# Two changes in the attention stage of a fused two-block kernel: sums of squares placed later in the order, and an output projection summed in four parts

## What is computed

```python
proj = h @ w_in                                   # od_w_in: 2048 x 4608
q, k, v, gate = split(proj)                       # 32 query heads, 4 key heads of 64
q = rope(rms_norm_2(q, q_norm_w), pos)            # needs a sum of squares per token and head
k = rope(rms_norm_2(k, k_norm_w), pos)
o = swa_sinks(q, k, v, sinks)                     # attention over a window of 128, with sinks
return (o * silu(gate)) @ w_out                   # od_w_out: 2048 x 2048, added to x
```

## Time and profile before

| | before |
|---|---|
| median of three runs | 1874.39 us |
| the profiled execution | 1875.87 us |
| its span, first to last instruction | 1874.0 us |
| TensorE busy | 1862.7 us, 99% of the span |
| VectorE busy | 1246.1 us, 66% |
| ScalarE busy | 1002.7 us, 54% |
| mean granted TensorE clock | 0.998 |

### The profile page before, as it was taken

The page is one execution under the profiler, slowest core; times in us unless marked ns, Lnnn a source line. Parts: engine busy times, 40 slices in busy tenths (PEclk is TensorE's granted clock), DMA queues, the critical chain, the costliest instruction groups (busy, mean ns, idle before and its releaser), DMA issues.

```text
span 1874.0 us, 22288 instructions
## 1 busy us (share of the span) xinstructions
PE 1862.7 (99%) x8403; PEld 1534.2 (82%) x8403; DVE 1246.1 (66%) x1833; ACT 1002.7 (54%) x1422; POOL 35.8 (2%) x90
## 2 busy tenths in 40 slices
PE   9999999999999999999999999999999999999999
PEld 7888888888888888888888888888888888877777
DVE  6676566776666556665466776765676666776786
ACT  6677554554444344443444455564565545476763
POOL 0001000000000000000000000000000001001100
PEclk9999999999999999999999999999999999999999
DMA  9667764786666666666666686666666678677985
GB/s 324 202 194 179 207 183 151 215 257 192 195 193 193 193 191 191 193 197 196 189 198 194 201 281 203 192 191 190 185 203 198 193 238 241 202 234 216 268 255 174
DMA packets 223628, 388.36 MB, mean 207 GB/s; under 512 B 15696, under 2 KB 45184, under 8 KB 223520
## 3 DMA queue, kind: packets, MB, share of 16 engines
q1 hardware_dynamic: 222272, 384.17, 68.3%
q0 software_dynamic: 816, 2.11, 0.8%
q10 hardware_dynamic: 432, 0.66, 0.1%
HBM read 367.83 MB, written 19.05 MB: 206 GB/s over the span
## 4 chain that ended last, share of the span: by engine, by line
PE 95%; DMA 2%; DVE 1%; ACT 1%; SPq 0%; issue 0%; DVEq 0%; ACTq 0%
PE g L1341 31%; PE g L1342 30%; PE g L1343 30%; DMA PTB<-probs 1%; DMA queries<-TWQ 1%; DVE wl L1797 1%; PE ob L1404 1%; ACT wh L1513 0%; DMA queries<-TE 0%; DMA probs<-A 0%; PE m L1391 0%; PE m L1483 0%; DMA A<-queries 0%; PE m L1283 0%; DVE TWQ L1797 0%
## 5 line engine op out<-in xcount | busy, mean ns | idle before, releaser
L1797 DVE TENSOR_TENSOR wl<-raw,wh 128x1024 fp32r<-128x1024 f32 (+1 forms) x660 | 802.0, 1216 | 554.1 <-ACT wh L1513 551.0
L1513 ACT ACTIVATE wh<-raw 128x1024 fp32r<-128x1024 f32 (+1 forms) x661 | 695.2, 1053 | 750.2 <-PE g L1343 739.5
L1341 PE MATMUL g<-wh,xh 128*128 128x512 f32 x1886 | 740.7, 393 | 0.0
L1343 PE MATMUL g<-wh,xl 128*128 128x512 f32 x1886 | 735.6, 390 | 0.0
L1342 PE MATMUL g<-wl,xh 128*128 128x512 f32 x1886 | 735.6, 390 | 0.0
L1341 PEld LDWEIGHTS g<-wh,xh 128*128 128x128 f32 x1886 | 354.5, 188 | 78.4 <-issue 3.8
L1343 PEld LDWEIGHTS g<-wh,xl 128*128 128x128 f32 x1886 | 354.5, 188 | 74.1
L1342 PEld LDWEIGHTS g<-wl,xh 128*128 128x128 f32 x1886 | 354.6, 188 | 72.2
L1341 PE MATMUL g<-wh,mh 128*128 128x512 f32 x732 | 287.6, 393 | 0.4 <-issue 0.4
L1343 PE MATMUL g<-wh,ml 128*128 128x512 f32 x732 | 285.4, 390 | 0.0
L1342 PE MATMUL g<-wl,mh 128*128 128x512 f32 x732 | 285.3, 390 | 0.0
(11 more groups left out here) (175 smaller groups left out, 716.3 us busy)
## 6 DMA issues: line engine op xcount, KB each, us to landing
raw<-in_ev_w_in SPq DMA_DIRECT2D x128, 512.0 KB, 3.8
raw<-in_w_in SPq DMA_DIRECT2D x92, 512.0 KB, 4.4
raw<-in_w_gate SPq DMA_DIRECT2D x88, 512.0 KB, 4.4
raw<-in_w_up SPq DMA_DIRECT2D x88, 512.0 KB, 4.4
raw<-in_w_down SPq DMA_DIRECT2D x88, 512.0 KB, 4.8
raw<-in_od_w_in SPq DMA_DIRECT2D x72, 512.0 KB, 4.5
raw<-in_w_out SPq DMA_DIRECT2D x32, 512.0 KB, 4.2
raw<-in_ev_w_out SPq DMA_DIRECT2D x32, 512.0 KB, 4.8
```

The source lines that it names most:

```text
L1341: e.matmul(o, hi[:, kt, c], h, start=first, stop=False)
L1343: last = e.matmul(o, lo[:, kt, c], h, start=False, stop=end)
L1513: return e.activation(o, i, AF.Copy, scale=scale)
L1797: return e.tensor_tensor(o, a, b, op)
```

## The change

Sums of squares of quarter j: `on_sum` is put into the order only when the planned end of the earlier quarter's send is 1.5 us past. The output projection's first part, rows 0 to 7, becomes two parts, rows 0 to 3 and rows 4 to 7; the moving of units ahead, which the first part had, falls away. The same weights are loaded and the same products made; there are 16 blocks of two units in place of four of four and eight of two, and so 16 `add` steps in place of 12.

```diff
-    for kts in (every[:8], every[8:12], every[12:]):
+    for kts in (every[:4], every[4:8], every[8:12], every[12:]):
         for j in range(4):
             block("od_w_out", 0, 512 * j, 512, kts, "M5", "add", j, kts[-1] == KT - 1, 4)
...
-    for acts, n in (("X1", 12), ("M3", 8), ("X2", 12), ("X3", 12), ("M5", 4)):
+    for acts, n in (("X1", 12), ("M3", 8), ("X2", 12), ("X3", 12)):
...
                     for i in range(2):
+                        while a[0] and self.end[("qsend", a[0] - 1, i)] + 1.5 > self.now:
+                            yield 1
                         say("on_sum", a[0], i)
```

## The result

The changed kernel takes 1877.54 us as a median of 12 runs, the kernel before 1874.66 in the 12 runs beside it: ratio 1.0015, 95% interval 1.0008 to 1.0022, some 2.9 us slower. The forecast was 1873.5, and its range ended at 1876.8. The prediction called less than 0.2% no change; the interval shows a loss all the same, where a small gain was forecast.

A forecast was written before the change was run, and what follows sets the result against it. TensorE, 99% busy, was taken as the bound, with idle and half clock around `oapv` 1. 1875.87 - 6.9 + 2.8 + 2.95 + 0.3 = 1875.0, less 1.48 for the median: 1873.5 us; own range 1871.5 to 1876, wider 1867.4 to 1876.8.

The forecast's parts named there:

- What bounds the kernel: TensorE, 99% busy; idle time and half clock around `oapv` of group 1 worth 0.69 + 3.25 + 2.95 = 6.9 us.
- Part one: Moving `on_sum` of quarter 2 later lets group 1's send and fetch leave earlier, removing the `oapv` 1 stretch: 6.9 us gained.
- with what drains earlier and the load that now comes behind, I take 1699.5: Landing of group 1's fetch, taken down from 1701.2; no wait left at `oapv` 1, bounds 0 and 2.0 us.
- the ring order: Earlier issue gains only the DMA engines' idle time: group 1's fetch lands at 1702.1, wait 1.7 us, sum 1.7 higher.
- The line set as refutation: A wait at `oapv` 1 above 2 us would refute part one.
- Part two: Four output-projection parts: counted adds push `oapv` 7 directly ahead of unit 653; 2.8 us more wait, 2.95 clock, 0.3 `pfetch` 5.
- The second turn's six looks for room: Group 6's second probability turn fails six planner checks for VectorE backlog (at most 3 us), placed six units later, delaying `oapv` 7.
- The clock: Half clock behind the late wait at unit 653 costs 2.95 us, bounds 0 and 2.95.
- clock holds: Rival: the wait at unit 653 ends before the clock falls; 1870.6 us, chance 0.17.
- The 0.3 us for `pfetch` 5: Allowance because group 5's fetch now goes out behind an add: 0.3 us, bounds 0 to 1.3.
- The third rival: Transfers queue behind others, `pfetch` of group 1 lands after 1702.8, clock falls again at `oapv` 1; 1879.8 us, chance 0.10.
- The upper end of 1876.8: Top of the wider range, 1867.4 to 1876.8 us, reaching to the bounds of the unknown costs.

The follow-up runs named there:

- e8: The changed kernel again, unaltered, run and profiled a second time: 1876.03 us, ratio 1.0020 to the kernel before.
- e1: The kernel before with part one alone (the wait ahead of `on_sum`), output projection still in three parts: 1872.65 us, ratio 0.9987.
- e7: Part one alone, with the two weight loads ahead of group 1's fetch (units 610 and 611) halved to 256 KB: 1870.88 us, one run.
- e4: Part one alone, with send and fetch of group 1's probabilities earlier in SyncE's order: 1870.01 us, ratio 0.9973 to the kernel before.
- e12: Part one alone, with only the fetch of group 1 moved ahead of the loads of units 610 and 611: 1870.05 us, ratio 0.9979.
- e11: The kernel before again, unaltered, profiled a second time: 1873.06 us, one run.
- e3: The changed kernel, both parts, with the output projection's adds made but left out of the planner's VectorE clock: 1871.41 us, ratio 0.9985.
- e10: The changed kernel without one look for room on VectorE, that of the second turn of group 6: 1880.51 us, one run.
- e2: The kernel before with part two alone (four parts of the output projection), `on_sum` in its old place: 1879.57 us, ratio 1.0022.
- e6: The changed kernel with adds not counted by the planner, and sends and fetches of groups 1 and 3 earlier: 1869.81 us, ratio 0.9980.
- e13: The kernel before, neither part, with only the fetch of group 1 moved ahead of the two loads: 1871.91 us, ratio 0.9987.
- e9: The changed kernel with adds not counted by the planner, and sends and fetches of groups 1, 3 and 5 earlier: 1870.74 us, ratio 0.9979.

## Why the prediction was wrong

**What bounds the kernel: right in kind, too large in size.** The stretch around `oapv` 1 was the place. Its worth of 6.9 us came from one execution; the second profile gives 4.9. The same kernel's send of the queries took 6.55 us in the one and 5.24 in the other, and the half clock cost 2.95 and 1.71 us.

**Part one: the step that failed is "with what drains earlier and the load that now comes behind, I take 1699.5".** The ends before it held: the send at 1684.75 for 1685.1, the fetch at 1691.52 for 1692.2. The landing came at 1701.35 in the first profile of the changed kernel, 1701.32 in the second (e8) and 1701.33 in e1; the 1701.2 that the prediction had before that last deduction was within 0.2 us of it. No load comes behind: the loads of units 610 and 611 stand ahead of the fetch in SyncE's queue before and after, as the earlier trace rows shows (0.96, x2). The 9.0 us from issue to landing already held their bytes, and there was nothing to take off; it measured 9.83. e7, e4 and e12 put these loads at 2.2 to 3.0 us each.

What an earlier issue gained was at most about the time in which the DMA engines had stood idle. Windows of the kernel before in its first profile, then in its second, e11 (columns as in the earlier trace rows):

```profile
1684.00:1688.00 4.00, 3.29 (x20) 2.16 (x20) 1.29 (x2) 1.62 (x3) 0.00 (x0) 1.00 0.72 275
1688.00:1692.00 4.00, 4.00 (x20) 3.30 (x19) 3.49 (x4) 3.12 (x6) 0.00 (x0) 1.00 0.57 129
```

```profile
1684.00:1688.00 4.00, 4.00 (x24) 2.93 (x19) 3.38 (x4) 1.82 (x5) 0.00 (x0) 1.00 0.67 204
1688.00:1692.00 4.00, 4.00 (x20) 3.30 (x19) 1.40 (x2) 3.97 (x5) 0.00 (x0) 1.00 0.87 307
```

The shares leave 2.8 us idle in the first and 1.8 in the second, an estimate from 0.72 and 0.57, 0.67 and 0.87; in the changed kernel the same eight microseconds are full (1.04 and 1.09). The landing gained 2.9 us against the first (1704.27) and 0.7 against the second (1702.02). Both agree with what I had drawn from the ring order in the Trainium skill ("DMA: Bandwidth & Descriptors", section "Queues, rings and completion order"): by it, with 2.2 us of idle time, the landing was 1702.1 and the wait 1.7; measured were 1701.35 and 2.18. I had weighed this case and set it aside for a value that no row gave. The line set as refutation, a wait above 2 us at `oapv` 1, was passed. Part one was worth 2.4 us (0.7 to 4.1), not 6.9.

TensorE came at 1699.2, not 1700.4: of that, 1.1 us are the head start at `oapv` 0, which the change did not make. It lengthened the wait, but cost no time, as the landing sets when `oapv` 1 begins.

**Part two: right in mechanism, and in the size of the late wait.** The planner's count of the adds was the cause (e3), `oapv` 7 fell directly ahead of unit 653, and the wait was 3.17 us in three profiles (3.2 forecast). Two steps inside it were off. The second turn's six looks for room are not the whole cause: the first turn stands three units later too (e10). And I gave no price to `oapv` 6, which falls between units 649 and 650 and waits 0.92, 0.64 and 1.16 us: the fetch of group 6 also has a load directly ahead of it, and took 8.8 us in the first profile.

**The clock: the term was mis-sized.** 2.95 us were taken over from the wait of 3.25 us. Measured behind 3.17 us: 1.5 us lost in the changed kernel, 1.6 in e2, none in e8. So the clock held behind this wait in one execution of three, as the rival "clock holds" had it. In sum part two was put at 6.05 us (2.8 + 2.95 + 0.3); e2 measured 4.1 (2.4 to 6.0).

**The 0.3 us for `pfetch` 5** had a real cause and too small a size. In all six profiles with four parts and this fetch in its place (changed, e2, e3, e6, e8, e10) it goes out 7.14 us after the send of group 5 left, although that send lands after 5.7 to 7.0 us; in the eight with three parts it goes out within 0.3 us of the landing. A load ahead of it needs a cut, and VectorE now makes an add before that cut. SyncE's queue of e8, where the send landed after 5.7 us:

```profile
1781.59 0.41 SPq L2458 DMA_DIRECT2D probs<-A  x1
1784.67 3.95 SPq L1269 DMA_DIRECT2D raw<-in_od_w_out  x2
1788.73 2.02 SPq L2467 DMA_DIRECT2D PTB<-probs  x4
```

So the add held the fetch for 0.1 to 1.4 us, and for 0.24 in the first profile of the changed kernel, where the send took 6.9. The rest of the 2.09 us at `oapv` 5 there goes with three transfers that were each 0.7 to 1.1 us longer than in the first profile of the kernel before. The wait was 1.45 us in e2, 0.56 in e10 and absent in e8, where TensorE came later; how much of it is the change's and how much the spread of the transfers, these runs don't tell.

**The rivals and the range.** The third rival, the first wait stays, was nearest: fetch queued behind others, landing 2.1 us behind TensorE's arrival, where I had put its point at 2.4. It had a chance of 0.10 and the time 1879.8, and the range cut it off. (Its gain forgone should be 6.2 us, 3.25 + 2.95, not 6.25.) The upper end of 1876.8 is not worked out there: the prediction's own bounds, 2.0 us at `oapv` 1, 5 at unit 653 and 1.3 for `pfetch` 5, would give 1878.3 together (2.0, 1.8 and 1.0 more than the sum holds), and the measured time lies below that. With the idle share as its only counter-argument, and two loads visible in the queue, it deserved more. Part one alone was put 4.5 us too high, more than the whole miss (1877.54 against 1873.5); part two, put 2.0 us too dear, gave some of it back, which was luck. Some 1.2 us of the miss are left over, as the changed kernel lost 2.9 us where e1 and e2 sum to 1.7; the intervals cover that.

## What to carry to other kernels

Where the DMA engines are full, look at what stands ahead of a late transfer in its queue, in bytes, before working on when it is issued: moving one fetch ahead of two loads took it from 9 or 10 us to 4 or 5 and gave as much as mending the chain in front of it. With part one beside it that gave the lowest ratio here, e4, 0.27% below the kernel before, without the four parts. A planner that counts a step which holds nothing up can still cost time through the order that it lays out; leaving the step out of the count showed that at once. And size a stall from two executions: here they gave 6.9 and 4.9 us.

## What the runs showed of the hardware

The drop of the granted clock didn't follow the length of the wait alone. Of the twenty waits of 1.67 us or more from the attention stage of the second block on (from 1640 us), in the fifteen profiles, fifteen ended in half clock and five did not. It fell after 1.67 us (e4, group 3) and 2.18 us, and held after 1.86 us (e3, group 1), 2.03 us (e13), 2.09 us (group 5 in the changed kernel), 2.37 us (e9, group 6) and once 3.17 us (e8); no wait of 1.45 us or less was followed by a drop. Where it fell, 0.50 lasted 3.4 or 6.8 us. The Trainium skill ("TensorE: Matmul & The Clock Gate", section "HAM oscillation — how this bites in real kernels") has products that wait for a DMA pay the return to half clock each time; here they paid most times, not each. Which of two equal waits is punished stays open: no run here separates what TensorE did in the microseconds around them.

Sends and fetches of the same bytes, in the same order, differed by up to 1.3 us between two executions of one kernel (the send of the queries, 6.55 and 5.24 us) and by 1.7 across kernels (the fetch of group 3 took 7.9 to 9.6 us where its place was left alone), and waits came and went at groups 3 and 5. Why, no run settles.
